# Two more slots for down weights in a two-layer mixer and expert network, with moved small buffers, scatters and transposes

## What is computed

```python
for l in range(DEPTH):
    h = rmsnorm(x, norm1_g[l]);  x = x + token_mixers(h, ..., w_in[l], ..., w_branch[l], w_out[l])
    h = rmsnorm(x, norm2_g[l]);  x = x + hierarchical_moe(h, ..., w_exp_gate[l], w_exp_up[l], w_exp_down[l])
return rmsnorm(x, norm_f_g)
# hierarchical_moe, for 128 tokens tb with combine weights cb:
a = einsum('td,edf->tef', tb, w_g);  u = einsum('td,edf->tef', tb, w_u)
hh = silu(a) * u * cb[:, :, None]
out = einsum('tef,efd->td', hh, w_d)
```

## Time and profile before

| | |
|---|---|
| median of 3 runs | 922.09 us |
| the profiled execution's own time | 921.21 us |
| its span, first to last instruction | 919.4 us |
| PE busy | 837.4 us, 91% |
| DVE, ACT, POOL busy | 529.3, 386.1, 115.7 us |
| data moved by DMA | 281.46 MB, mean 306 GB/s |
| mean granted clock of TensorE | 0.963 |
| mixer of layer 0, experts of layer 0 | about 4 to 255 us, 255 to 458 us |
| mixer of layer 1, experts of layer 1 | about 458 to 706 us, 706 to 909 us |

### The profile page before, as it was taken

How to read it: one execution, slowest core, us unless ns; L and a number is a source line. 1 busy time by engine, 2 the same in 40 slices (tenths; PEclk the granted TensorE clock), 3 DMA queues, 4 the chain that set the end, 5 groups by cost and what they waited for, 6 DMA issues and landing times.

```text
span 919.4 us, 20305 instructions
## 1 busy us (share of the span) xinstructions
PE 837.4 (91%) x8771; PEld 668.2 (73%) x8771; DVE 529.3 (58%) x1067; ACT 386.1 (42%) x667; POOL 115.7 (13%) x169
## 2 busy tenths in 40 slices
PE   7999889999999998877899997999999999878884
PEld 6997778887887765554589976888789876645652
DVE  5667679667545553433366676785756455434424
ACT  6546767645512221211265567684544222211113
POOL 3730101221000000000165001021300000000000
PEclk9999999999999999998999998999999999979878
DMA  9975444585899999999997453445859999999994
GB/s 306 380 200 167 135 156 141 180 343 206 326 383 419 420 417 421 419 420 419 400 362 250 137 182 104 159 147 214 371 182 367 410 418 419 419 420 420 422 419 163
DMA packets 63836, 281.46 MB, mean 306 GB/s; under 512 B 5088, under 2 KB 7216, under 8 KB 39168
## 3 DMA queue, kind: packets, MB, share of 16 engines
q1 hardware_dynamic: 62464, 278.45, 77.5%
q0 software_dynamic: 800, 1.40, 1.0%
q10 hardware_dynamic: 480, 0.28, 0.1%
HBM read 279.06 MB, written 1.05 MB: 305 GB/s over the span
## 4 chain that ended last, share of the span: by engine, by line
PE 53%; DMA 21%; DVE 8%; ACT 6%; issue 5%; SPq 3%; POOL 2%; DVEq 0%; POOLq 0%; ACTq 0%
DMA ring<-in_w_exp_up 12%; PE ps L462 10%; PE ps L464 9%; PE ps L463 9%; PE ps L780 7%; DMA late<-in_w_exp_up 6%; PE ps L767 4%; PE ps L794 4%; DMA late<-in_w_exp_down 3%; DVE split_lo L1602 2%; SPq L366 2%; PE ps L875 2%; ACT split_hi L1069 2%; POOL wide L1489 1%; PE ps L429 1%
## 5 line engine op out<-in xcount | busy, mean ns | idle before, releaser
L1602 DVE TENSOR_TENSOR split_lo<-ring,split_hi 128x1024 fp32r<-128x1024 f32 (+1 forms) x142 | 195.2, 1415 | 44.8 <-ACT split_hi L1069 41.4
L462 PE MATMUL ps<-split_hi,hT_hi 128*128 128x512 f32 (+2 forms) x416 | 162.8, 391 | 14.2 <-DVE split_lo L1602 11.6
L464 PE MATMUL ps<-split_hi,hT_lo 128*128 128x512 f32 (+2 forms) x416 | 159.6, 384 | 0.0
L463 PE MATMUL ps<-split_lo,hT_hi 128*128 128x512 f32 (+2 forms) x416 | 159.1, 382 | 0.0
L1069 ACT ACTIVATE split_hi<-ring 128x1024 fp32r<-128x1024 f32 (+1 forms) x140 | 141.5, 1052 | 26.3 <-PE ps L464 26.1
L2006 DVE TENSOR_TENSOR br<-br,ps 32x64 f32<-32x64 f32 x256 | 54.9, 215 | 149.3 <-ACT br L1288 146.7
L1288 ACT ACTIVATE br<-ps 128x64 f32<-128x64 f32 x64 | 14.3, 224 | 252.1 <-PE ps L780 252.1
L462 PEld LDWEIGHTS ps<-split_hi,hT_hi 128*128 128x128 f32 x416 | 79.4, 191 | 33.6 <-DVE split_lo L1602 16.5
L464 PEld LDWEIGHTS ps<-split_hi,hT_lo 128*128 128x128 f32 x416 | 79.1, 190 | 14.8
L463 PEld LDWEIGHTS ps<-split_lo,hT_hi 128*128 128x128 f32 x416 | 79.6, 191 | 13.5
L1506 POOL TENSOR_TENSOR idx<-idx,wt 128x128 f32<-128x128 f32 x32 | 12.1, 400 | 401.9 <-PE ps L800 318.4
(11 more groups left out here) (275 smaller groups left out, 1309.2 us busy)
## 6 DMA issues: line engine op xcount, KB each, us to landing
ring<-in_w_in SPq DMA_DIRECT2D x52, 1024.0 KB, 6.8
ring<-in_w_exp_gate SPq DMA_DIRECT2D x45, 1024.0 KB, 25.6
ring<-in_w_exp_up SPq DMA_DIRECT2D x45, 1024.0 KB, 26.0
late<-in_w_exp_down SPq DMA_DIRECT2D x45, 1024.0 KB, 26.5
ring<-in_w_exp_down SPq DMA_DIRECT2D x19, 1024.0 KB, 26.7
new_pair<-in_w_exp_gate SPq DMA_DIRECT2D x10, 1024.0 KB, 23.3
new_pair<-in_w_exp_up SPq DMA_DIRECT2D x10, 1024.0 KB, 25.2
late<-in_w_exp_gate SPq DMA_DIRECT2D x9, 1024.0 KB, 24.1
```

Source lines behind the costliest of these rows:

```text
L462: mm(dst, st[0], mv[0], start=start, stop=False, skip_group_check=True)
L463: mm(dst, st[0], mv[1], start=False, stop=False, skip_group_check=True)
L464: return mm(dst, st[1], mv[0], start=False, stop=stop, skip_group_check=True)
L1602: V.tensor_tensor(half_view(split_lo[:, v % SPLITS, :], v), raw_half(v, l), half_view(split_hi[:, v % SPLITS, :], v).bitcast(F32), ALU.sub ...
```

## The change

Two more buffers take down weights. `tmpP` and `vl` become one buffer `first_down`, which takes the down weights of expert 0 alone (name "first"), and `br` (name "br") becomes one of now 8 slots that the other experts go round. What lay in `br` moves: `scatT` to `wr`, `hid` to `wsT`, `silu` and `hidT` to `mb`, the routing values to `yy`, one column to `scal`. The loads' order is written anew: 16 first loads in place of 14, then gate and up of experts 7 to 10 before the next down (9). PE scatters each of the last three experts behind the down product of the next one (before, expert 28 was so placed already). In layer 1 the transposes of x come quarter by quarter, tile by tile; the third quarter stands behind the matmuls of tile 0, the fourth behind those of tile 2. At the start 6 warming matmuls stand in place of 13, and 3 new ones before the first weights. POOL's first low parts of layer 1 wait for `down_mm` 28 in place of 31.

```diff
-DOWNS = (("att", "yT", "lo0", "lo1", 8, "hT1", "hT0"), ("att", 8, "yT", "lo0", "lo1", "hT1", "hT0"))
-RP, RD = 7, 7
+DOWNS = (("hT1", "hT0", "lo0", "lo1", 8, "yT", "att", "br"), ("att", 8, "br", "yT", "lo0", "lo1", "hT1", "hT0"))
+RP, RD = 7, 8
...
-FIRST_LOADS = ((("gu", 1), ("gu", 2), ("d", 0), ("gu", 0), ("gu", 4), ("gu", 5), ("gu", 6), ("d", 4), ("d", 1), ("gu", 3),
-                ("d", 2), ("d", 3), ("d", 5), ("d", 6)),
-               (("gu", 0), ("gu", 1), ("d", 0), ("gu", 2), ("gu", 3), ("gu", 4), ("d", 1), ("gu", 5), ("d", 2), ("gu", 6),
-                ("d", 3), ("d", 4), ("d", 5), ("d", 6)))
-NEXT_LOADS = [("gu", RP + k) for k in range(2)]
-for _e in range(RD, NE):
+FIRST_LOADS = ((("gu", 1), ("d", 0), ("gu", 2), ("d", 7), ("gu", 0), ("gu", 4), ("gu", 5), ("d", 8), ("gu", 6), ("d", 5),
+                ("d", 6), ("d", 1), ("gu", 3), ("d", 3), ("d", 4), ("d", 2)),
+               (("gu", 0), ("d", 0), ("gu", 1), ("d", 1), ("gu", 2), ("gu", 3), ("gu", 4), ("d", 3), ("d", 2), ("gu", 5),
+                ("d", 4), ("gu", 6), ("d", 5), ("d", 6), ("d", 7), ("d", 8)))
+NEXT_LOADS = [("gu", _e) for _e in range(RP, RD + 3)]
+for _e in range(RD + 1, NE):
     if _e + 2 < NE:
         NEXT_LOADS.append(("gu", _e + 2))
     NEXT_LOADS.append(("d", _e))
...
+def down_name(e, l):
+    return DOWNS[l][(e - 1) % RD] if e else "first"
...
-        tmpP = sb("tmpP", [P, TT, 512])
+        first_down = sb("first_down", [P, UNIT])
+        tmpP = first_down[:, 0:HALF].rearrange("p (t n) -> p t n", t=TT)
...
-        vl = sb("vl", [P, 2, TT, BW])
+        vl = first_down[:, HALF:].rearrange("p (k t n) -> p k t n", k=2, t=TT)
...
-                keep_warm(13, 3)
+                keep_warm(6, 3)
...
                         x_transposes(1, 0, C)
+                        keep_warm(3, 0)
                     else:
-                        for k in range(4):
+                        def x_quarter(k):
                             pe.wait_ge(*layer_count(l - 1)(x_add, 4 * GROUPS - 3 + k))
-                            for t in range(TT):
-                                x_transposes(t, 2 * k, 2 * k + 2)
-                    in_unit(0, 0)
+                            for c in (2 * k, 2 * k + 1):
+                                for t in range(TT):
+                                    x_transposes(t, c, c + 1)
+
+                        x_quarter(0)
+                        x_quarter(1)
+                    if l == 0:
+                        in_unit(0, 0)
+                    else:
+                        in_half(0, 0, "natural", lambda: x_quarter(2))
+                        in_half(1, 0, "natural", lambda: x_quarter(3))
...
-                        if e >= NE - 2:
+                        down_expert(e)
+                        if e > LASTG:
                             scatter_expert(e - 1)
-                        down_expert(e)
-                        if e == LASTG + 1:
-                            scatter_expert(LASTG)
...
+                        elif name == "first":
+                            sp.wait_ge(*L(pv_mm, 2))
+                            sp.wait_ge(*L(vn_done, 1))
+                        elif name == "br":
+                            sp.wait_ge(*L(gate_prod, 8))
...
-                        pool.wait_ge(*last(down_mm, NE - 1))
+                        pool.wait_ge(*last(down_mm, max(e for e in range(NE) if down_name(e, l - 1) == "lo0") + 1))
```

More of the change, by code:

```diff
@@ L196, in build @@
         brf = br[:, :, :, :].rearrange("p a b n -> p (a b n)")
[L197 to L205, removed]
+        scatT = wr[:, :, :].rearrange("p c e -> p (c e)")[:, 0:2 * P].rearrange("p (t s) -> p t s", t=TT)
+        hid = wsT[:, :, :].rearrange("p g s -> p (g s)")[0:SLOTS, :].rearrange("p (a f) -> p a f", a=2)
+        silu = mb[:, 0:128].rearrange("p (a f) -> p a f", a=2)
+        hidT = mb[:, 128:256].rearrange("p (a k s) -> p a k s", a=2, k=2)
+        yyf = yy[:, :, :, :].rearrange("p a t n -> p (a t n)")
+        rl = yyf[:, 512:512 + TT * 36].rearrange("p (t e) -> p t e", t=TT)
+        member = yyf[:, 640:704].rearrange("p (t e) -> p t e", t=TT)
+        prod32 = yyf[:, 704:768].rearrange("p (t g e) -> p t g e", t=TT, g=NG)
+        rt = yyf[:, 768:1024]
+        cnts = scal[:, 56:57]
         ps = ctx.enter_context(nc.psum_tensor("ps", [P, 8, 512], F32))
@@ L215, in build @@
         d_loaded = [sem(f"d_loaded{i}") for i in range(RD)]
+        first_loaded = sem("first_loaded")
         x_loaded1 = sem("x_loaded1")
@@ L333, in down_slot @@
         def down_slot(e, l):
-            name = DOWNS[l][e % RD]
+            name = down_name(e, l)
+            if name == "first":
+                return first_down[:]
+            if name == "br":
+                return brf
             if name in LATE_AT:
@@ L344, in d_loads @@
         def d_loads(e, l):
-            return (d_loaded[e % RD], 16 * (l * len(range(e % RD, NE, RD)) + e // RD + 1))
+            if e == 0:
+                return (first_loaded, 16 * (l + 1))
+            k = (e - 1) % RD
+            return (d_loaded[k], 16 * (l * len(range(k + 1, NE, RD)) + (e - 1) // RD + 1))
         def gu_bank(e):
@@ L370, in load_down @@
             sp.dma_start(down_slot(e, l).rearrange("p (k d) -> p k d", k=2),
[L371 removed]
+                         w_ed_v[l * NE + e]).then_inc(d_loads(e, l)[0], 16)
         x_pair, x_down = ring[:, MRING * UNIT:(MRING + 2) * UNIT], ring[:, (MRING + 2) * UNIT:]
@@ L478, in emptied, with in_half @@
                             pe.wait_ge(*L(tr_out, k - 1))
-                    def in_half(v, use, layout):
+                    def in_half(v, use, layout, between=None):
                         b0 = 2 * (use % 2)
@@ L513, in in_half @@
                                                 end and k == 1)
+                                if k == 0 and between is not None:
+                                    between()
                         else:
@@ L1004, in _ @@
                             if s_ in DOWNS[l]:
-                                last = max(e for e in range(NE) if DOWNS[l][e % RD] == s_)
+                                last = max(e for e in range(NE) if down_name(e, l) == s_)
                                 sp.wait_ge(*L(down_mm, last + 1))
```

2 lines of the change are left out of this document (1 added, 1 removed).

## The result

The changed kernel took 910.49 us (median of 4 runs, 909.75 to 912.79), the kernel before 922.3 us (919.6 to 923.9) beside it: ratio 0.9875, 95% interval 0.9854 to 0.9897. That is 11.8 us less. Predicted were 910.1 us, 906.4 to 915.2. The sum held; two of its terms did not, in opposite directions, and the runs show by how much.

The account below looks back on a forecast made before the run. It took DMA to bound the expert parts, PE the mixers, with serial starts and ends. Terms -1.5 - 5.0 - 0.4 + 1.7 - 5.0 - 0.9 gave -11.1 us, from 921.21 to 910.1 us; range 906.4 to 915.2.

Parts of the forecast that it names:

- Two slots: Expert parts: two MB more per layer load in idle DMA time before the DMA-full stretch, 5.0 us saved a layer.
- PE's waits in the two buffers: Expert parts, both layers: PE's waits for gate and up weights should fall from 32.9 to some 25 us.
- (b): Expert parts: one pair of MB not hidden, or PE the limit in one layer; 5.0 us lost, 915.1 us, chance 0.09.
- (d): Mixer loads: "br" or "first" held until other gates open, so only start and scatters gain; 920.1 us, chance 0.03.
- The other loads keep the number of those that wait for the mixer's end: First loads: six MB wait before and six now, leaving 73 MB instead of 75 from the first recycled slot on.
- Scatters: End of each layer: down products fill PE's 0.64 us idles before the last two scatters; -0.4 us layer 0, -0.9 layer 1.
- The landing of down 31: End of layer 0: the last expert's down weights land at about 453.9 us, so PE waits shortly for DMA.
- The start: Program start: less warming ahead of x's transposes brings the first product sooner; -1.5 us, between 0 and -2.2.
- The interleaved start of layer 1: Start of layer 1: fourth quarter's transposes come later and delay ACT's chain and unit 2; +1.7 us, bounds -0.3 to +3.4.
- Rival (a): Start of layer 1: interleaving costs nothing, as later work absorbs the slip of ACT's chain; 908.4 us, chance 0.13.
- rival (c): Start of either layer: PE's clock steps down where it did not before, one step costing 1.6 us; 911.7 us, chance 0.10.

Follow-up runs that it names:

- the run with the late load: Changed kernel with the load into br placed last of the first loads, not behind the eighth gate product: 913.35 us, 0.9895 of the kernel before.
- the quarters first: Changed kernel with all four quarters of x transposed before layer 1's first product, as in the kernel before: 908.57 us, 0.9846 of the kernel before.
- the early table alone: Changed kernel with all quarters of x transposed first and ACT's square-root table loaded ahead of the high parts: 910.21 us, 0.9865 of the kernel before.

## Why the prediction was right, and where it was not

- **Two slots, -5.0 a layer.** Right: -5.1 and -5.0 in the two traces, 186.1 to 186.5 us in all 24 stretches (two layers of twelve traces) with br loaded early, and the whole gain is there when the slots stand alone. The mechanism held as written: idle windows of the earlier trace rows filled, PE's waits in the two buffers down by 6.1 us (some 8 were forecast), in all three by 5.3. Rivals (b) and (d) fall.
- **What I took from it and should not have.** "The other loads keep the number of those that wait for the mixer's end" was read as if DMA had been full from there on. The stretch from 262.60 was; the 1.5 us before it were not, as the run with the late load shows.
- **Scatters, -0.4 and -0.9.** The sum of 1.3 was nearly right (0.75 each, 1.5). In layer 0 the term was -0.4 and measured -0.7. The landing of down 31 was not at fault: I had it 7.5 us behind the start of gate and up 31 (453.9 - 446.36), and PE started down 31 at 7.53 (449.15 - 441.62). PE's waits for down weights add up to the 0.8 us that I had, as 0.17, 0.23 and 0.40. What was too long is the tail behind it, 1.07 + 2 x 1.15 = 3.37 us in my sum, 3.01 measured (449.15 to 450.15 + 2.01): the last two scatters run on as one of 2.01. In layer 1 the old order took 11.6 us in the trace of before with a pause of PE of 0.35 us in it, 11.3 without; the change measured -0.8 without that pause, where I had -0.9.
- **The start, -1.5.** 12 warming records took 2.93 us, not 2.5. The first product came 1.2 sooner, measured against the profiled execution of before. But that trace has an early rise of the clock; with a late one the first product comes at 14.0 us behind 13 warming matmuls, and the edit is then worth 2.3, just outside my bound of 2.2. I had priced the transposes at both levels, and the warming that goes only as the earlier trace rows had it.
- **The interleaved start of layer 1, +1.7.** Mechanism and place right (ACT's last high parts 1.8 us later, PE waits at both ends); 16.2 us to unit 2 against 14.4 before and 14.2 with the quarters first, so +1.9. Missed was what the delay would run into: POOL's DMA issue and memset, 1.4 us more in two of six traces. That this stayed inside my upper bound of +3.4 is luck: the bound was priced for a clock step, and a clock step in this stretch costs the interleaved start nothing (16.2 us with it and without). Rival (a) falls. The sentence that the chain on ACT is the bound was half of it: with quarters first PE's 48 products are as long, and the early table alone has nothing to shorten.
- **The clock, rival (c).** Layer 0's mixer took 1.5 us longer in the trace of the changed kernel, from a dip of the granted clock in another place.

Two windows of layer 0's mixer in the kernel before (PEclk is the third number from the end):

```profile
105.00:115.00 10.00, 7.46 (x35) 6.24 (x34) 6.90 (x8) 6.15 (x6) 1.31 (x2) 0.83 0.22 67
118.00:128.00 10.00, 7.63 (x44) 6.43 (x43) 8.19 (x12) 6.90 (x10) 0.00 (x0) 1.00 0.32 105
```

The second one in the changed kernel:

```profile
118.00:128.00 10.00, 7.82 (x31) 6.38 (x31) 7.96 (x12) 5.29 (x7) 0.00 (x0) 0.83 0.40 115
```

0.83 over 10 us is 3.4 us at 1.2 GHz. The kernel before had them in the first window: its products from 110.57 to 117.54 took 1.1 us longer than those of the changed kernel (109.37 to 115.21), but PE's next wait was 1.1 us shorter (2.37 for 3.44), so nothing was lost. The changed kernel had them in the second: its products from 120.18 to 127.36 took 7.2 us against 5.6 (121.38 to 126.95), and no wait gave that back. So the step exists, as rival (c) said, but the change does not make it: this mixer took 231.9 us in three traces (the kernel before and two variants) with low clock near 110 us only, and 233.4 to 234.0 in eight (the variants with 13 warming matmuls among them) with a stretch near 120. The last three took 232.4, with low clock near 110 and 250. Layer 1's mixer spreads in the same way, from 231.7 to 234.0. The low clock in the start of layer 1 is not made by the interleaving either: two of the four traces with the quarters first have it.

The forecast of 910.1 was thus right partly by luck: the start was worth up to 0.8 us more than said, the start of layer 1 cost 0.2 to 1.6 more, and these cancel in part. Added up with the values of the runs: -2.3 (start) - 10.1 - 1.5 + 1.9 is -12.0, with the stall (+3.3) -10.6; measured were -11.8.

## What to carry to other kernels

When transfers bound a stretch, a buffer is worth its transfer time only as far as its load falls where the DMA engines stand still; look for every such gap, also the short one ahead of the first recycled slot. Before work is interleaved into a start, follow who feeds the longest chain: the order that starts PE soonest was 1.9 us slower (in traces without low clock there), and grouping both late transposes behind one tile, with a table load moved into idle time, was 4.2 us faster than the changed kernel (how much each of the two gives is not separated). Below some 3 us a median can't price an edit here; a stretch between two marks in several traces can.

## What the hardware showed that I had not expected

- A one-source DVE operation of 0.28 us took 1.9 us where POOL had begun a DMA issue 0.0 to 0.1 us earlier, with a memset behind it; with POOL 0.02 us later there was no loss. Six traces hold nothing between 16.2 and 17.6 us.
- The first rise of TensorE's clock comes at different moments for the same warming matmuls, read from their durations (7.8 us in the trace of before; not before 9.9 us in another). The granted clock reads 1.00 through all of it.
- Stretches of 3.4 us at 1.2 GHz come in both mixers in every trace, at a few fixed places of the program, in varying choice. Their price is by place: nothing where PE waits anyway, 1.6 us near 120 us, some 0.5 at 250, 1.3 to 1.7 in the start of layer 1 when its products bound it. Together that is about as much as the up to 6 us between runs of one kernel (919.6 to 925.6 for the kernel before), though where the low stretches lay is known of profiled executions alone.
